# Moving ScalarE roundings ahead of a PSUM copy, and one sigmoid and one finishing step inside a pair loop, in the input projection of a hybrid encoder layer

## The chip, the cores and the metric

The kernel runs on one core of a Trainium2 chip. The metric is the device time in microseconds (us), the median over runs. TensorE (PE) multiplies, VectorE (DVE) and ScalarE (ACT) work on tiles in SBUF and PSUM, GpSimd (POOL) issues stores, SyncE (SP) issues loads.

## The reference

One encoder layer over 1024 prompt tokens and 256 sample tokens, all in float32. What matters here is its first product:

```
h = rms_norm(x, g_mix);  proj = h @ w_in        # (1280, 1024) @ (1024, 4096)
hq, hf_fwd, hf_bwd, hi, hg, dq, dk, dv = split(proj)      # eight groups of 512 columns
q_hg = silu(hq);  gate = silu(hg)
f = lb + (1 - lb) * sigmoid(hf);  lf = log(f);  k = 1 - f       # for hf_fwd and for hf_bwd
```

After it come a gated linear scan (HGRN2), differential attention, cross attention to 256 memory tokens, and a mixture of experts. None of that is changed.

## The kernel before

The function `front` computes the projection. Each float32 operand is split into a rounded high part and the low rest, and each product is three matmuls (`product3`, lines 113 to 115). ACT writes the high part and DVE subtracts it to get the low part.

**The steps.** The groups that are stored by token (`v`, `g`, `dv`) take 15 steps, n = 0 to 14, of two token tiles each: 48 matmuls of 512 columns into one of two PSUM halves, `acc[:, n % 2]`. PE may begin step n when the half has been read (`acc_read[n % 2]` at n // 2). In the steps of `dv`, n = 10 to 14, it is ACT that reads it, in `copy_out(n)` (line 516).

**The preparation of the pairs.** The other groups are stored by column. Ten pairs p = 0 to 9 (`q` 0 and 1, `f_fwd` 2 and 3, `f_bwd` 4 and 5, `dq` 6 and 7, `dk` 8 and 9) of 256 columns are computed as a two by two block product with seven products. They need four sums of token blocks, S1 to S4. DVE forms one with three additions over 128x2048 (`combine`, lines 709 to 713), ACT rounds it (`round_s`, line 526) and DVE subtracts (`low_s`, line 718). During steps 10 to 14 these are made, along with the eight weight slots of pair 0 (`round_slot` on ACT, line 538; `low_slot` on DVE, line 733). All engines run their instructions in the order in which the code lists them, with semaphores between them.

**The pairs.** For pair p, PE does eight slots in order, among them slots for the sample tokens (256 columns wide, into `x_t`). Before slot 7 it waits for `u3_done` of the same pair, since `p4_ps` and `p7_ps` are one bank: DVE must have added `p7_ps` to `partial` (`make_u3`, line 753). Meanwhile ACT and DVE make the slots of pair p + 1 and finish the chunks of pair p. Five chunks, c = 0 to 4, go through `clamp(p, c)` on DVE (line 797), `sigmoid(p, c)` on ACT (exponential, logarithm, exponential on lines 561 to 565, and for pairs 2 to 5 the logarithm of line 574 too), and `finish(p, c)` on DVE (line 805, or 808 for pairs 2 to 5). Pairs 6 to 9 have no sigmoid. `round_next(p, i)` is the rounding of slot i of pair p + 1; slots 4 and 7 wait for differences that DVE forms in `prepare(p + 1, 4)` (lines 745 and 746). The order on ACT for one p is:

```
copy_p1; sigmoid(p - 1, 3); sigmoid(p - 1, 4); round_next 0, 1; sigmoid(p, 0);
round_next 2, 3; sigmoid(p, 1); round_next 4, 5; copy_sample; round_next 6; sigmoid(p, 2); round_next 7
```

Of the kernel before, what the change touches and what calls it, by code (L numbers as in the profile page):

```python
# [171 lines left out]
def front(nc, tag, sources, gain, hg_lb, lam_vecs, ident, eps, lb, one_minus_lb, lb_minus_one, lam, weight, out,  # L172
# [26 lines left out]
    first_step = [g * tiles for g in range(len(BY_TOKEN))]  # L199
# [12 lines left out]
    S1, S3, S2, S4 = range(1, 5)  # L212
    with Mem(nc, tag) as m:
# [93 lines left out]
        def wait_pair_raw(eng, p):  # L307
            if p == 0:
                eng.wait_ge(first_pair_in, 16)
            else:  # L310
                eng.wait_ge(pair_in[p % 2], 16 * ((p + 1) // 2))
# [29 lines left out]
        with nc.Block() as block:  # L341
# [118 lines left out]
            def _(act):  # L460
# [16 lines left out]
                def find_mem_rstd(j):  # L477
                    t = NT + j
                    act.wait_ge(x_in[0], 16 * (NT // 2 + j + 1))
                    act.wait_ge(turned, t)  # L480
                    act.activation(xn[0][:], x[0][:], ACT.Square, accum_out=ss[:, t:t + 1])
                    act.drain()
                    act.activation(rstd[:, t:t + 1], ss[:, t:t + 1], ACT.Ln, scale=1.0 / D, bias=eps[:, 0:1])
                    act.drain()
                    act.activation(rstd[:, t:t + 1], rstd[:, t:t + 1], ACT.Exp, scale=-0.5).then_inc(rstd_done, 1)
# [38 lines left out]
                def round_s(i):  # L524
                    act.wait_ge(s_raw_done, i)
                    act.activation(s[i][:, 0], s_raw[i][:], ACT.Copy).then_inc(s_high_done, 1)

                def round_slot(p, i):
                    if i == 0:
                        wait_pair_raw(act, p)  # L530
                    if p:
                        act.wait_ge(slot_used, 8 * (p - 1) + i + 1)
                    elif i == 0:
                        act.wait_ge(mm_done, first_step[2])
                    made = {2: 2, 3: 1, 4: 3, 7: 4}
                    if i in made:
                        act.wait_ge(t_done, 4 * p + made[i])
                    act.activation(slot[:, i, 0], slot_source(p, i), ACT.Copy).then_inc(slot_high_done, 1)

                def round_next(p, i):  # L540
                    if p < last_pair:
                        round_slot(p + 1, i)
# [7 lines left out]
                def copy_sample(p):  # L550
                    act.wait_ge(sample_ready, p + 1)
                    wait_chunk_free(act, p, 2)
                    act.activation(chunk_of[:, 2], sample_ps(p), ACT.Copy, scale=scale_of(p)).then_inc(sample_copied, 1)

                def sigmoid(p, c):
                    if not 0 <= p < sig_pairs:
                        return
                    n = chunk_no(p, c)
                    part = sig[:, n % 3]
                    act.wait_ge(part_clamp_done, n + 1)  # L560
                    act.activation(part, part, ACT.Exp, scale=-1.0)
                    act.drain()
                    act.activation(part, part, ACT.Ln, bias=one[:, 0:1])
                    act.drain()
                    act.activation(part, part, ACT.Exp, scale=-1.0).then_inc(part_sig_done, 1)
                    if pairs[p][0] in GATES:
                        g = gate_no(p, c)
                        act.drain()
                        if g == 0:
                            act.wait_ge(lb_done, 1)  # L570
                        if g >= 3:
                            act.wait_ge(lf_stored[g % 3], 16 * (g // 3))
                        for h, cols in heads_of(p, c):
                            done = act.activation(staged_lf[:, g % 3, cols], part[:, cols], ACT.Ln,
                                                  scale=one_minus_lb[:, h:h + 1], bias=lb[:, h:h + 1])
                        done.then_inc(lf_done, 1)
# [26 lines left out]
                for n, (g, kind, j) in enumerate(steps):  # L603
                    if n < tiles:
                        continue
                    if n in chunk_in_step:
                        round_chunk(chunk_in_step[n])
                    if first_mem < n <= first_mem + mem_tiles:
                        round_mem(n - first_mem - 1)
                    if first_mem <= n < first_mem + mem_tiles:  # L610
                        find_mem_rstd(n - first_mem)
                    if kind in SILUS:
                        wide_sigmoid(n)
                    else:
                        copy_out(n)
                    if n == first_step[2]:
                        round_s(S1)
                    if n == first_step[2] + 1:
                        for i in range(8):
                            round_slot(0, i)  # L620
                        round_s(S3)
                    if n == first_step[2] + 3:
                        round_s(S2)
                    if n == first_step[2] + 4:
                        round_s(S4)
                    for r in out_rounds.get(n, ()):
                        round_out(r)

                for p in range(len(pairs)):
                    copy_p1(p)  # L630
                    sigmoid(p - 1, 3)
                    sigmoid(p - 1, 4)
                    round_next(p, 0)
                    round_next(p, 1)
                    sigmoid(p, 0)
                    round_next(p, 2)
                    round_next(p, 3)
                    sigmoid(p, 1)
                    round_next(p, 4)
                    round_next(p, 5)  # L640
                    if p == last_pair:
                        act.wait_ge(next_in, 32)
                        act.wait_ge(slot_used, 8 * p + 3)
                        for i, (_, high_of, _) in enumerate(next_split):
                            act.activation(high_of[:], next_raw[:, i], ACT.Copy).then_inc(next_high_done, 1)
                    copy_sample(p)
                    round_next(p, 6)
                    sigmoid(p, 2)
                    round_next(p, 7)

            @block.vector
            def _(dve):
# [83 lines left out]
                def prepare(p, *which):  # L736

                    if p > last_pair:
                        return
                    for i in which:  # L740
                        if i == 1:
                            differences(p)
                        if i == 4:
                            dve.drain()
                            dve.tensor_tensor(spread[:, 1], weights_of(p, 1, 0), spread[:, 1], ALU.subtract)
                            dve.tensor_tensor(spread[:, 0], weights_of(p, 1, 1), weights_of(p, 0, 1),
                                              ALU.subtract).then_inc(t_done, 1)
                            dve.drain()
                            dve.sem_inc(t_done, 1)
                        low_slot(p, i)  # L750
# [131 lines left out]
                for p in range(len(pairs)):  # L882
                    finish(p - 1, 3)
                    prepare(p + 1, 0)
                    finish(p - 1, 4)
                    prepare(p + 1, 1)
                    make_c11(p)
                    clamp(p, 0)
                    make_u2(p)
                    prepare(p + 1, 2)  # L890
                    make_u3(p)
                    make_c22_u4(p)
                    clamp(p, 1)
                    prepare(p + 1, 3)
                    finish(p, 0)
                    prepare(p + 1, 4, 5)
                    clamp(p, 2)
                    if p == last_pair:
                        for i, (_, high_of, low_of) in enumerate(next_split):
                            dve.wait_ge(next_high_done, i + 1)  # L900
                            dve.tensor_tensor(low_of[:], next_raw[:, i], high_of[:].bitcast(F32), ALU.subtract)
                    make_c12(p)
                    clamp(p, 3)
                    finish(p, 1)
                    prepare(p + 1, 6)
                    make_c21(p)
                    clamp(p, 4)
                    finish(p, 2)
                    prepare(p + 1, 7)
# [2468 lines left out]
```

## Time and profile before

| | |
|---|---|
| median of 3 runs | 2049.55 us (2048.66 to 2050.41) |
| profiled execution, its own time | 2048.66 us |
| its span in the trace | 2046.9 us |
| granted TensorE clock, mean | 0.984 |
| PE busy | 1956.1 us, 96% |
| DVE busy | 1489.8 us, 73% |
| ACT busy | 1237.7 us, 60% |
| first matmul of pair 0 | 201.22 us from the start of the span |
| first matmul after `front` | 460.38 us |

Times in the trace count from the start of the span. The timeline gives each instruction's start, then its duration, then engine, line, operation and tiles; in brackets stands how long its engine sat idle before it, and what released it. A matmul is recorded as 0.39 us long, but they follow each other at 0.227 us.

### The profile page before, as it was taken

To read this page: it belongs to the slowest core of one execution; us is meant where nothing else is said; L and a number is where in the kernel's file an instruction comes from. 1 tells how busy PE (TensorE), PEld (TensorE's weight loads), DVE (VectorE), ACT (ScalarE), POOL (GpSimd) and SP (SyncE) were. 2 spreads that over 40 slices of the span, in tenths; PEclk is the share of its full clock that TensorE was granted. 3 is DMA by queue.
4 is the path that set the end of the run, shared out by engine and by line. 5 is a ranking of instruction groups with operands and counts; after the bars stand their busy time and mean duration, and the time that the engine had idled before them with its cause. 6 is when DMAs were issued, how large, how long until landed. Compare 5 with 4: busy or idle time off the path is not lost. (4 is left out here: it accounts for less than half of the span.)

```text
span 2046.9 us, 31859 instructions
## 1 busy us (share of the span) xinstructions
PE 1956.1 (96%) x11162; PEld 1618.9 (79%) x11162; DVE 1489.8 (73%) x2050; ACT 1237.7 (60%) x1974; POOL 307.8 (15%) x394
## 2 busy tenths in 40 slices
PE   7989999999999899999998999999999999999983
PEld 6878887888888676778887888887888888888871
DVE  5447766639999588887311455579999999999976
ACT  5443566418787598643222333337888888888863
POOL 0220012200000121111000000011222332222210
PEclk9999999999999999999999999989999999999997
DMA  6493233446554541343335322448999999999988
GB/s 209 165 308 109 93 124 134 160 170 200 175 173 156 188 160 60 97 144 133 117 115 164 124 103 73 165 170 317 383 384 382 380 379 375 384 383 395 376 314 321
DMA packets 178389, 448.27 MB, mean 219 GB/s; under 512 B 21152, under 2 KB 100384, under 8 KB 151648
## 3 DMA queue, kind: packets, MB, share of 16 engines
q1 hardware_dynamic: 146032, 347.48, 47.6%
q0 software_dynamic: 32240, 99.25, 13.1%
q8 instruction: 70, 1.15, 0.2%
q14 instruction: 47, 0.39, 0.1%
HBM read 366.46 MB, written 94.90 MB: 225 GB/s over the span
## 5 line engine op out<-in xcount | busy, mean ns | idle before, releaser
L113 PE MATMUL cross_ot_ps<-w_w_high,cross_o_high 128*128 128x512 f32 x544 | 219.8, 404 | 2.1 <-DVE w_w_low L2933 1.6
L115 PE MATMUL cross_ot_ps<-w_w_high,cross_o_low 128*128 128x512 f32 x544 | 213.3, 392 | 0.0
L2933 DVE TENSOR_TENSOR cross_low_up<-cross_raw_up,w_w_high 128x2048 fp32r<-128x2048 f32 x68 | 152.8, 2289 | 12.3 <-ACT w_w_high L2717 12.2
L2933 DVE TENSOR_TENSOR cross_low_down<-cross_raw_down,w_w_low 128x2048 fp32r<-128x2048 f32 x68 | 152.7, 2288 | 1.8 <-ACT w_w_low L2717 1.7
L2933 DVE TENSOR_TENSOR w_w_low<-cross_raw_gate,w_w_high 128x2048 fp32r<-128x2048 f32 x68 | 152.2, 2278 | 0.0
L2717 ACT ACTIVATE w_w_high<-cross_raw_up 128x2048 fp32r<-128x2048 f32 x68 | 126.2, 1907 | 0.3 <-issue 0.3
L2717 ACT ACTIVATE w_w_low<-cross_raw_down 128x2048 fp32r<-128x2048 f32 x68 | 126.2, 1907 | 0.0
L2717 ACT ACTIVATE w_w_high<-cross_raw_gate 128x2048 fp32r<-128x2048 f32 x68 | 126.1, 1902 | 0.0
L113 PEld LDWEIGHTS cross_ot_ps<-w_w_high,cross_o_high 128*128 128x128 f32 x544 | 102.9, 189 | 28.5 <-DVE w_w_low L2933 7.1
L115 PEld LDWEIGHTS cross_ot_ps<-w_w_high,cross_o_low 128*128 128x128 f32 x544 | 102.7, 189 | 22.2
L113 PE MATMUL cross_out_ps<-w_w_low,cross_ht 128*128 128x512 f32 x272 | 109.5, 403 | 5.6 <-DVE cross_low_down L2933 5.6
L114 PE MATMUL cross_ot_ps<-w_w_low,cross_o_high 128*128 128x512 f32 x272 | 107.0, 393 | 0.0
L115 PE MATMUL cross_out_ps<-w_w_low,cross_ht 128*128 128x512 f32 x272 | 107.0, 393 | 0.0
L114 PE MATMUL cross_out_ps<-cross_low_down,cross_ht 128*128 128x512 f32 x272 | 106.6, 392 | 0.0
L114 PE MATMUL cross_ot_ps<-cross_low_up,cross_o_high 128*128 128x512 f32 x272 | 106.0, 390 | 0.0
L2627 POOL COPY cross_result<-cross_result_i 128x1 int32 x32 | 39.7, 1239 | 332.0 <-ACT cross_x L2753 332.0
L1782 DVE CUSTOM_DVE_ANT_0 amq_score<-amq_banks,amq_bias 128x1024 f32<-128x1024 f32 x64 | 75.8, 1221 | 14.2 <-PE amq_banks L2177 13.9
L2631 POOL DMA_INDIRECT y_rows<-cross_x,cross_result x32 | 81.9, 2559 | 27.0 <-POOL cross_result L2627 27.0
L2744 ACT ACTIVATE cross_o_high<-cross_score_ps 128x1024 fp32r<-128x1024 f32 x34 | 34.9, 1028 | 82.4 <-PE cross_score_ps L3252 82.4
L2196 PEld LDWEIGHTS amq_banks<-amq_v,amq_attn_t 128*128 128x128 f32 x512 | 59.6, 191 | 25.4 <-ACT amq_attn_t L1985 20.8
L1977 ACT ACTIVATE amq_prob<-amq_score,amq_least 128x1024 f32<-128x1024 f32 x64 | 72.6, 1137 | 4.9 <-DVE amq_least L1782 4.9
L113 PEld LDWEIGHTS cross_out_ps<-w_w_low,cross_ht 128*128 128x128 f32 x272 | 51.5, 189 | 23.6 <-issue 10.4
(515 smaller groups left out, 5570.2 us busy)
## 6 DMA issues: line engine op xcount, KB each, us to landing
cross_raw_gate<-in_w_gate_dram SPq DMA_DIRECT2D x68, 1024.0 KB, 7.0
cross_raw_down<-in_w_down_dram SPq DMA_DIRECT2D x68, 1024.0 KB, 7.7
cross_raw_up<-in_w_up_dram SPq DMA_DIRECT2D x68, 1024.0 KB, 9.0
front_pair_raw<-in_w_in_dram SPq DMA_DIRECT2D x9, 1024.0 KB, 7.0
cross_y_kept<-y_rows SPq DMA_DIRECT2D x16, 512.0 KB, 9.4
front_raw<-in_w_in_dram SPq DMA_DIRECT2D x10, 512.0 KB, 5.3
k_t<-front_staged POOLq DMA_DIRECT2D x20, 256.0 KB, 2.4
lf_t<-front_staged_lf POOLq DMA_DIRECT2D x20, 256.0 KB, 3.2
```

Source lines behind the costliest of these rows:

```text
L113: pe.matmul(out, lhs[0], rhs[0], start=first, stop=False)
L114: pe.matmul(out, lhs[0], rhs[1], start=False, stop=False)
L115: return pe.matmul(out, lhs[1], rhs[0], start=False, stop=last)
L1782: done = dve.tensor_tensor_reduce(out=score[:, u, c], in0=score_ps[:, c], in1=bias[:, h, col:col + SEQ_P], scale=1.0, scalar=3.0e38, op0=A ...
L1977: done = act.activation(prob[:, u, c], score[:, u, c], ACT.Exp, scale=-1.0, bias=least[:, u, c:c + 1], accum_out=total[:, n % 4, c:c + 1])
L2196: last = pe.matmul(o_ps[:, u, 0:P], attn_t[:, c * P:(c + 1) * P], v[:, c, h * P:(h + 1) * P], start=(c == 0), stop=(c == NT_P - 1))
L2627: pool.tensor_copy(result[u][:], result_i[:, ds(n, 1)]).then_inc(result_done, 1)
L2631: pool.indirect_dma_start(out=y_rows, in_=y[:, u], in_offset=None, out_offset=bass.IndirectOffsetOnAxis(ap=at, axis=0), bounds_check=2 * T ...
L2717: act.activation(w_high[s][:, cols], raw[s][:, cols], ACT.Copy).then_inc(w_high_done[s], 1)
L2744: act.activation(x_high[:, u].rearrange("p k t -> p (k t)"), xt_ps[:], ACT.Copy).then_inc(x_high_done, 1)
L2933: dve.tensor_tensor(w_low[s][:, cols], raw[s][:, cols], w_high[s][:, cols].bitcast(F32), ALU.subtract).then_inc(w_low_done[s], 1)
```

## The change

Three orders are changed; no instruction is added or taken away.

```diff
@@ ScalarE, steps n = 10 to 14
                     if first_mem <= n < first_mem + mem_tiles:
                         find_mem_rstd(n - first_mem)
+                    if n == first_step[2]:
+                        round_s(S1)
+                    if n == first_step[2] + 1:
+                        round_s(S3)
+                        for i in range(8):
+                            round_slot(0, i)
+                    if n == first_step[2] + 3:
+                        round_s(S2)
+                    if n == first_step[2] + 4:
+                        round_s(S4)
                     if kind in SILUS:
                         wide_sigmoid(n)
                     else:
                         copy_out(n)
-                    if n == first_step[2]:
-                        round_s(S1)
-                    if n == first_step[2] + 1:
-                        for i in range(8):
-                            round_slot(0, i)
-                        round_s(S3)
-                    if n == first_step[2] + 3:
-                        round_s(S2)
-                    if n == first_step[2] + 4:
-                        round_s(S4)
@@ ScalarE, the pair loop
                     round_next(p, 2)
                     round_next(p, 3)
-                    sigmoid(p, 1)
                     round_next(p, 4)
                     round_next(p, 5)
...
                     copy_sample(p)
+                    sigmoid(p, 1)
                     round_next(p, 6)
@@ VectorE, the pair loop
                     make_u2(p)
-                    prepare(p + 1, 2)
+                    finish(p, 0)
+                    prepare(p + 1, 2, 3)
                     make_u3(p)
                     make_c22_u4(p)
                     clamp(p, 1)
-                    prepare(p + 1, 3)
-                    finish(p, 0)
                     prepare(p + 1, 4, 5)
```

`first_step[2]` is 10, the first step of `dv`.

## Rows read from the trace of the kernel before

**Rows 1.** Waits, 160 to 465 us: engine, line, releaser, us in total, times, longest

```profile
PE front_acc L113 <- DVE front_partial L753: 5.4, 3, 3.0
```

**Rows 2.** Timeline of PE: firsts of steps 12 and 14, and of slots in pairs

```profile
167.56 0.39 PE L113 MATMUL front_acc<-front_w_high,front_bottom 128*128 128x512 f32 x1
...
190.19 0.50 PE L113 MATMUL front_acc<-front_w_high,front_sample 128*128 128x512 f32 x1 [0.71 <-ACT front_staged L516]
...
201.22 0.39 PE L113 MATMUL front_acc<-front_top,front_slot 128*128 128x512 f32 x1
...
223.34 0.39 PE L113 MATMUL front_acc<-front_bottom,front_slot 128*128 128x512 f32 x1
...
226.06 0.39 PE L113 MATMUL front_acc<-front_top,front_slot 128*128 128x512 f32 x1
...
299.36 0.47 PE L113 MATMUL front_acc<-front_bottom,front_slot 128*128 128x512 f32 x1 [1.33 <-DVE front_partial L753]
...
302.19 0.39 PE L113 MATMUL front_acc<-front_top,front_slot 128*128 128x512 f32 x1
...
327.47 0.77 PE L113 MATMUL front_acc<-front_bottom,front_slot 128*128 128x512 f32 x1 [3.00 <-DVE front_partial L753]
...
331.88 0.40 PE L113 MATMUL front_acc<-front_top,front_slot 128*128 128x512 f32 x1
...
358.03 0.39 PE L113 MATMUL front_acc<-front_top,front_slot 128*128 128x512 f32 x1
```

**Rows 3.** Busy time by stretch; after the engines: granted clock, DMA share, GB/s

```profile
320.00:330.00 10.00, 7.00 (x33) 5.72 (x32) 6.62 (x12) 4.51 (x8) 0.13 (x1) 0.87 0.15 54
```

**Rows 4.** Timeline of ACT during steps 10 to 14

```profile
156.98 1.01 ACT L516 ACTIVATE front_staged<-front_acc 128x1024 f32<-128x1024 f32 x1
170.17 1.92 ACT L526 ACTIVATE front_s<-front_s_raw 128x2048 fp32r<-128x2048 f32 x1 [12.18 <-DVE front_s_raw L713]
171.99 1.01 ACT L516 ACTIVATE front_staged<-front_acc 128x1024 f32<-128x1024 f32 x1
...
187.33 1.90 ACT L526 ACTIVATE front_s<-front_s_raw 128x2048 fp32r<-128x2048 f32 x1
189.14 1.92 ACT L516 ACTIVATE front_staged<-front_acc 128x1024 f32<-128x1024 f32 x2
```

**Rows 5.** Timeline of ACT in the pairs, pair 4 above all

```profile
233.12 0.62 ACT L561 ACTIVATE front_sig<-front_sig 128x512 f32<-128x512 f32 x1
...
256.89 0.62 ACT L561 ACTIVATE front_sig<-front_sig 128x512 f32<-128x512 f32 x1
...
283.02 0.62 ACT L561 ACTIVATE front_sig<-front_sig 128x512 f32<-128x512 f32 x1
...
311.13 0.62 ACT L561 ACTIVATE front_sig<-front_sig 128x512 f32<-128x512 f32 x1
...
325.21 1.13 ACT L538 ACTIVATE front_slot<-front_spread 128x512 fp32r<-128x512 f32 x2
329.26 0.63 ACT L561 ACTIVATE front_sig<-front_sig 128x512 f32<-128x512 f32 x1 [2.92 <-DVE front_sig L797]
...
332.19 0.61 ACT L538 ACTIVATE front_slot<-front_spread 128x512 fp32r<-128x512 f32 x1
...
338.41 0.57 ACT L548 ACTIVATE front_partial<-front_acc 128x512 f32<-128x512 f32 x1
338.89 0.62 ACT L561 ACTIVATE front_sig<-front_sig 128x512 f32<-128x512 f32 x1
```

**Rows 6.** Timeline of DVE in pair 4

```profile
326.64 0.69 DVE L753 SCALAR_TENSOR_TENSOR front_partial<-front_acc,front_partial 128x512 f32<-128x512 f32 x1
...
328.80 0.43 DVE L797 TENSOR_SCALAR front_sig<-front_staged 128x512 f32<-128x512 f32 x1
329.14 0.69 DVE L733 TENSOR_TENSOR front_slot<-front_spread,front_slot 128x512 fp32r<-128x512 f32 x1
...
330.99 0.68 DVE L746 TENSOR_TENSOR front_spread<-front_pair_raw 128x512 f32<-128x512 f32 x1
```

## The prediction, made before the changed kernel ran

> **What bounds the kernel.** I read the page first: TensorE is busy for 96% of the span, so a change in the order of the other engines counts only where TensorE has to wait. The view of the waits, cut to the stretch from 160 to 465 us in which the change lies, shows how little there is: the reader is to see that three waits on DVE's `partial` make 5.4 us [rows 1], and the timeline adds one of 0.71 us on ACT's copy, at the start of step 14 [rows 2]. Everything else runs at the pace of the matmuls: 48 in a step at 0.227 us are 10.88 us; one pair takes 226.06 - 201.22 = 24.84 us, and reaches slot 7 at 223.34 - 201.22 = 22.12 us [rows 2]. Pairs 0, 1 and 2 keep this pace, so pair 3 starts at 201.22 + 3 x 24.84 = 275.74. Pair 6 starts at 358.03 instead of 275.74 + 3 x 24.84 = 350.26: pairs 3, 4 and 5 lose 7.77 us. That is the three pauses, and the clock after the longest. The granted clock is 0.87 from 320 to 330 us [rows 3], a mixture of the two levels of 1.2 and 2.4 GHz. The twelve matmuls after the 3.00 us pause take 331.88 - 327.47 = 4.41 us for 2.72, a loss of 1.7; after the pause of 1.33 us they take 302.19 - 299.36 = 2.83, a loss of 0.1 [rows 2].
>
> So I looked for two things: which instruction the edits put between TensorE and what it waits for, and how long the loop between ACT and DVE takes per pair.
>
> **Edit 1, ACT in steps 10 to 14.** Before, ACT copies step 10 out at 156.98, and only then waits 12.18 us for DVE's last addition of S1, so that the rounding starts at 170.17 [rows 4]. After, `round_s(S1)` stands ahead of that copy. Nothing makes the addition earlier: DVE had been waiting for the stores of `out_split`, on which the copy has no bearing. The rounding stays at 170.17, the next instruction on ACT starts at 171.99, and this is now the copy of step 10, done at 173.00 as the copy in that place was. TensorE needs it for step 12 (`acc_read[0]` at 6), which was to start at 167.56 [rows 2]. It starts at 173.05: 5.5 us late.
>
> Then step 11. ACT rounds S3 (1.9 us) when DVE has added it up, and then the eight slots, paced by DVE's subtractions and differences as before; they end so that the next instruction starts at 187.33, where the rounding of S3 stood [rows 4]. Now the copy of step 11 starts there, and ends 1.01 us later at 188.34. TensorE needs it for step 13. Step 12 would end at 173.05 + 10.88 = 183.93 plus what the clock costs after the pause (1.7 as after the pause of 3.00), 185.6. So there is a second wait, of some 2.7 us, and step 13 starts at 188.38 whatever the clock did before. The 0.71 us ahead of step 14 goes away, since the copy of step 12 now comes at 188.3 and not at 189.14. Steps 13 and 14 take 2 x 10.88 plus the clock's loss after the second wait. That pause is between the ones of 1.33 and 3.00, so the loss is between 0.1 and 1.7, and I take 1.0. Pair 0 starts at 188.38 + 21.76 + 1.0 = 211.1 instead of 201.22: **9.9 us late**, with bounds of 9.0 and 10.6. The roundings of S2 and S4 ahead of the copies of steps 13 and 14 cost nothing here: S2 is rounded about when step 13 ends, and pair 0 needs the copy of step 14 only for its fourth slot. If those sums were late, TensorE would wait in pair 0 for `s_ready` too. Queued behind the held copies are POOL's stores of `dv_rows` and, since `mm_done` comes later, SP's loads for pairs 1 and 2; both move with TensorE.
>
> **Edits 2 and 3, the pair loop.** I measure ACT's loop from the first exponential of `sigmoid(p - 1, 3)`. Pair 4 to pair 5 is 338.89 - 311.13 = 27.76 us, pair 3 to pair 4 is 28.11 [rows 5]. Both are longer than TensorE's 24.84, and this is why TensorE waits. In the loop, DVE's `u3` starts at 326.64, 15.51 after the loop's start, and ends at 327.33, which releases slot 7 at 327.47 [rows 2, 6].
>
> After: `finish(p, 0)` fits into the time in which DVE waits for ACT's rounding of slot 2 at 325.21 [rows 5] and costs nothing. The subtraction of slot 3 moves ahead of `u3`. In the old order it stood behind `clamp(p, 1)` at 329.14, and the rows there follow each other at 0.6 us [rows 6]. So `u3` comes 0.6 later, and so does the clamp: 329.4. The differences that slot 4 needs ended at 330.99 + 0.68 = 331.67; with 0.6 more ahead of the clamp and 1.2 less behind it (and a drain of 0.1 in its place) they end at 331.2. The rounding of slot 4 was at 332.19 behind a sigmoid, and is now at 331.25: 0.9 earlier only, while the sigmoid of 2.93 us (332.19 - 329.26) now comes after it. ACT waited 2.92 us for the clamp; it now waits for the differences, 5 us. From the rounding of slot 4, the four short instructions of 0.52, 0.52, 0.48 and 0.52, the sigmoid of 2.93, `sigmoid(p, 2)` of 3.21, slot 7 of 0.52 and the copy of 0.48 lead to the next start at 340.43 for 338.89: **the loop becomes 1.54 us longer, 29.3 us**. In pair 2 the same walk gives 283.02 - 256.89 = 26.13 before and 27.7 after. In pairs 0 and 1, without the second logarithm, 256.89 - 233.12 = 23.77 before and 24.8 after [rows 5], just TensorE's pace.
>
> Against this stands that TensorE starts pair 0 late, and so the loop less far behind it. Before, the loop's start in pair 2 was 256.89 - 250.90 = 6.0 us after TensorE's. After, it is as near as it can be: twelve matmuls (2.72), 0.2, and the copy at 338.41 to 338.89 (0.48) [rows 5], 3.4 us. Then pair 3: 3.4 + 27.7 - 24.84 = 6.2 us behind. Slot 7 of pair 5 can start no sooner than 6.2 + 2 x 29.3 + 15.51 + 0.6 + 0.69 + 0.14 = 81.8 us after TensorE's start of pair 3; without waits it would be 2 x 24.84 + 22.12 = 71.8. That is 10.0 us lost, and behind it 1.2 of clock (bounds again 0.1 and 1.7): 11.2 for 7.77 before, so **3.4 us more**, with bounds of 2.3 and 3.9. The clock's losses at the earlier pauses don't add to it, since they shorten the next pause. If the loads for pair 1 hold the loop up, it starts up to 1.9 us further behind, and the upper bound is 5.8. Pairs 6 to 9 have hardly any work for ACT and catch up.
>
> **The sum.** 9.9 + 3.4 = 13.3 us. After `front` every stage starts on TensorE's end, so the rest moves as a whole. The profiled execution's own time of 2048.66 becomes 2062.0; the median of 2049.55, 0.9 above it, becomes 2062.9.
>
> [...]
>
> **Rivals.**
> - *The pair loop doesn't get longer* (the sigmoid's place is taken up by ACT's idle time, as the edit would suggest). Then only the nearer start counts: 3.4 + 26.13 - 24.84 = 4.7 behind, slot 7 of pair 5 at 4.7 + 2 x 27.76 + 16.34 = 76.6 for 71.8, with the clock 6.0 lost for 7.77. Total 9.9 - 1.8 = 8.1, 2057.7 us. Against it: the differences, which ACT then waits for, are only 0.5 us earlier.
> - *The loop starts as far behind as before*, 6.0 or more, because of the loads. Then 2.6 us more, 2065.5.
> - *The pair loop's pauses vanish altogether*, if rounding slots 4 and 5 early were what `u3` hangs on: 9.9 - 7.8 = 2.1, 2051.7 us. Against it: `u3` waits for slot 2's subtraction, which is not earlier.
> - *Not slower: the copy of step 10 is not held.* Place: ACT, ahead of step 12. It decides if DVE's last addition of S1 ends before the copy could start at 156.98 and the slots' roundings before 178.4. Then 1.0 us is gained ahead of step 14, and with a loop of the old length and the nearer start another 1.8: 2046.7 us, 0.14% under the time before. Against it: the addition ends 13 us too late, and no edit touches what it waits for.
>
> **How the numbers follow.** Forecast 0.62; loop not longer 0.13; loop as far behind 0.15; pauses gone 0.04; copy not held 0.03; and 0.03 left for what I don't see, most of it on the side of faster. A measurement of this kernel can tell about 0.2% (4 us) from no change. The pauses gone (0.10% slower) and the copy not held both count as the same. So slower 0.90, same 0.07, faster 0.03. The range: the low bounds give 9.0 + 2.3 = 11.3, so 2060.9, the high ones 10.6 + 5.8 = 16.4, so 2066.0. I stretch it down to 2058, which the shorter loop nearly reaches, and up to 2067.
>
> **What would show it.** In the profile after: a wait of TensorE for ACT's line of `copy_out` near 173 us and a second near 188, of 5.3 and some 2.5 us, and none ahead of step 14; the rounding of S1 still at 170.2; pair 0's first matmul near 211; ACT's loop at 29.3 us in pairs 3 and 4; pauses ahead of slot 7 of about 1, 4 and 2.5 us in pairs 3 to 5, released by `partial`; the first matmul after `front` near 473.7. It is wrong if step 12 starts near 167.6, or if the loop stays at 27.8.

## The result, and the profile after

The changed kernel took 2064.74 us (median of 3 runs, 2061.48 to 2066.44) for 2049.55: a ratio of 1.0073, with a 95% interval from 1.0054 to 1.0091. It is slower, as forecast, and the time lies in the range. Its profiled execution took 2061.51 us, with a span of 2059.7 for 2046.9, 12.8 us more. The forecast was 13.3. The medians lie further apart than the profiled executions, 15.2 us; the runs of one kernel scatter by 4 to 5 us, and a part of the experiments is about where.

What TensorE waited for from 160 to 480 us, in the profile after:

```profile
PE front_acc L113 <- DVE front_partial L753: 7.9, 3, 4.2
PE front_acc L113 <- ACT front_staged L516: 7.8, 2, 5.3
```

The waits for ACT's copy grew from 0.7 to 7.8 us, and those for `partial` from 5.4 [rows 1] to 7.9. The timeline of PE, with the rows that answer to [rows 2]:

```profile
172.84 0.80 PE L113 MATMUL front_acc<-front_w_high,front_bottom 128*128 128x512 f32 x1 [5.33 <-ACT front_staged L516]
...
188.20 0.50 PE L113 MATMUL front_acc<-front_w_high,front_bottom 128*128 128x512 f32 x1 [2.48 <-ACT front_staged L516]
...
199.21 0.39 PE L113 MATMUL front_acc<-front_w_high,front_sample 128*128 128x512 f32 x1
...
210.09 0.39 PE L113 MATMUL front_acc<-front_top,front_slot 128*128 128x512 f32 x1
...
259.77 0.39 PE L113 MATMUL front_acc<-front_top,front_slot 128*128 128x512 f32 x1
...
284.61 0.39 PE L113 MATMUL front_acc<-front_top,front_slot 128*128 128x512 f32 x1
...
307.82 0.47 PE L113 MATMUL front_acc<-front_bottom,front_slot 128*128 128x512 f32 x1 [0.92 <-DVE front_partial L753]
...
337.14 0.76 PE L113 MATMUL front_acc<-front_bottom,front_slot 128*128 128x512 f32 x1 [4.23 <-DVE front_partial L753]
...
366.48 0.47 PE L113 MATMUL front_acc<-front_bottom,front_slot 128*128 128x512 f32 x1 [2.77 <-DVE front_partial L753]
...
370.80 0.50 PE L113 MATMUL front_acc<-front_top,front_slot 128*128 128x512 f32 x1
...
473.27 0.64 PE L113 MATMUL hgrn_acc<-mem_high,mem_next_high 128*128 128x512 f32 x1 [2.83 <-PEq L91]
```

Step 12 starts at 172.84 for 167.56, step 13 at 188.20, and step 14 at 199.21 without a wait. Pair 0 starts at 210.09 for 201.22: 8.9 us. From the start of pair 3 to that of pair 6 it is 370.80 - 284.61 = 86.19 us, which is 11.7 more than three times 24.84; before it was 7.8 more. The first matmul after `front` comes at 473.27 for 460.38: 12.9 us, and that is the whole difference of the spans. The granted clock (after the engines) in the stretch with the longest pause of the pairs is 0.84 for 0.87 [rows 3]:

```profile
330.00:340.00 10.00, 5.77 (x21) 4.38 (x20) 7.17 (x13) 3.84 (x6) 1.07 (x2) 0.84 0.21 80
```

ACT in the steps, answering to [rows 4]:

```profile
155.83 1.06 ACT L522 ACTIVATE front_out_high<-front_out_raw 128x1024 fp32r<-128x1024 f32 x1 [5.38 <-DMA front_out_raw<-in_w_out_dram]
169.97 1.91 ACT L526 ACTIVATE front_s<-front_s_raw 128x2048 fp32r<-128x2048 f32 x1 [13.08 <-DVE front_s_raw L713]
171.78 1.00 ACT L516 ACTIVATE front_staged<-front_acc 128x1024 f32<-128x1024 f32 x1
176.90 1.93 ACT L526 ACTIVATE front_s<-front_s_raw 128x2048 fp32r<-128x2048 f32 x1 [4.11 <-DVE front_s_raw L713]
...
187.15 1.92 ACT L516 ACTIVATE front_staged<-front_acc 128x1024 f32<-128x1024 f32 x2
```

The copy of step 10 was at 156.98 and is now at 171.78, behind a rounding that waits 13.08 us. The copies of steps 11 and 12 follow each other from 187.15. ACT in the pairs, answering to [rows 5] (the loop of pair 2 starts at 263.19, that of pair 4 at 320.22 and the next at 349.54):

```profile
263.19 0.62 ACT L561 ACTIVATE front_sig<-front_sig 128x512 f32<-128x512 f32 x1
...
320.22 0.62 ACT L561 ACTIVATE front_sig<-front_sig 128x512 f32<-128x512 f32 x1
...
334.27 1.13 ACT L538 ACTIVATE front_slot<-front_spread 128x512 fp32r<-128x512 f32 x2
340.38 0.63 ACT L538 ACTIVATE front_slot<-front_spread 128x512 fp32r<-128x512 f32 x1 [4.97 <-DVEq L748]
...
341.91 0.62 ACT L561 ACTIVATE front_sig<-front_sig 128x512 f32<-128x512 f32 x1
...
349.54 0.62 ACT L561 ACTIVATE front_sig<-front_sig 128x512 f32<-128x512 f32 x1
```

In pair 2 the loop starts 263.19 - 259.77 = 3.42 us behind TensorE, for the 3.4 of the prediction. In pair 4 it takes 29.32 us for 27.76. The wait of 2.92 us for the clamp is gone, and one of 4.97 for DVE's differences stands in its place, with the sigmoid behind it at 341.91. DVE in the same pair, answering to [rows 6]:

```profile
333.50 0.55 DVE L808 TENSOR_SCALAR front_staged<-front_sig,kept_lb_minus_one,kept_one_minus_lb 128x512 f32<-128x512 f32 x1 [1.41 <-ACT front_sig L565]
334.92 1.29 DVE L733 TENSOR_TENSOR front_slot<-front_spread,front_slot 128x512 fp32r<-128x512 f32 x2 [0.86 <-ACT front_slot L538]
336.30 0.69 DVE L753 SCALAR_TENSOR_TENSOR front_partial<-front_acc,front_partial 128x512 f32<-128x512 f32 x1
...
339.60 0.69 DVE L746 TENSOR_TENSOR front_spread<-front_pair_raw 128x512 f32<-128x512 f32 x1
```

`finish(p, 0)` at 333.50 lies in DVE's wait for slot 2, as predicted, with 0.86 us to spare. Two subtractions (334.92, x2) now stand ahead of `u3`, at 336.30 - 320.22 = 16.08 us from the loop's start for 15.51. The differences end at 340.29, 20.1 from it, for 20.5.

### The profile page after: what moved, and what is told of

The parts are those of the page before. It is cut to its first block and busy times, and to the rows that moved or that the text cites. A ratio compares the mean times of both kernels' runs of the same rounds, so it can differ in the third digit from the quotient of the medians.

```text
span 2059.7 us, 31859 instructions
## 1 busy us (share of the span) xinstructions
PE 1958.7 (95%) x11162; PEld 1620.1 (79%) x11162; DVE 1491.5 (72%) x2050; ACT 1237.7 (60%) x1974; POOL 307.7 (15%) x394
```

## The experiments

Times below are medians, and a ratio, with its 95% interval, is against runs of the kernel before that were taken beside it (medians of 2050.07, 2049.66 and 2049.53 us). "Front end" is the first matmul after `front`, 460.38 us before. It is read from one profiled execution. For what the edits do inside `front` it is the better measure, for a reason that the first run shows; it says nothing of what follows.

**The change once more.**

> The changed kernel once more. Its profiled execution took 2061.5 us, 12.9 more than the one before, and its timed runs had a median of 2064.7, 15.2 more. If the clock's loss after the middle pauses differs from run to run (bounds 0.1 and 1.7 us at each of two), five rounds scatter between 2061.5 and 2065 and the ratio is 1.006 to 1.0075. If the profiled execution was a lucky one, they all lie at 2064 and above.

2062.35 us (2061.68 to 2066.63), ratio 1.0061, 1.0046 to 1.0076. The profiled execution took 2066.63, 5.1 us longer than the one above. Its `front` ended at 473.29, as the other one did at 473.27. So the difference between these two executions arises behind `front`. These five runs lie in two bunches, near 2062 and near 2066; of the three above, one (2064.74) lies between. I had looked for the scatter in the pauses of the pairs, and it is elsewhere.

That the two front ends agree to 0.02 us is partly chance. In this execution steps 12 and 13 and pair 0 start some 0.55 us later (pair 0 at 210.65), and behind the third pause of the pairs the clock costs 0.1 us where it cost 1.7. What evens it out is that slot 7 of pair 6 waits here for `u3`, which it did not do above:

```profile
367.04 0.47 PE L113 MATMUL front_acc<-front_bottom,front_slot 128*128 128x512 f32 x1 [2.60 <-DVE front_partial L753]
...
392.95 0.47 PE L113 MATMUL front_acc<-front_bottom,front_slot 128*128 128x512 f32 x1 [0.81 <-DVE front_partial L753]
```

Pair 0 itself starts between 200.50 and 201.51 us in the five profiles in which the orders of the steps are those of before. So a difference of a microsecond between two front ends can be chance, and where the clock behind a pause is in it, one of 1.6.

The 5 us of the whole execution lie further on. The largest part lies where the experts start: the first transposes there (before 1380 us) came 0.8 us later in the longer execution, the first matmul of the experts at 1384.9 for 1382.0, and the second block's transposes at 1400.43 for 1396.47. There, busy time and granted clock (the column behind POOL) in the execution of 2061.5 us:

```profile
1380.00:1384.00 4.00, 4.00 (x21) 3.50 (x21) 3.78 (x6) 0.00 (x0) 0.00 (x0) 0.67 0.88 329
1384.00:1388.00 4.00, 4.00 (x18) 3.25 (x17) 3.88 (x3) 0.00 (x0) 0.00 (x0) 0.90 0.75 264
1388.00:1392.00 4.00, 4.00 (x24) 3.39 (x23) 2.78 (x6) 2.03 (x3) 0.99 (x1) 1.00 0.96 371
```

and in the one of 2066.6:

```profile
1381.00:1385.00 4.00, 4.00 (x21) 4.00 (x20) 3.67 (x6) 0.00 (x0) 0.00 (x0) 0.50 0.93 340
1385.00:1389.00 4.00, 4.00 (x11) 3.13 (x11) 3.99 (x2) 0.00 (x0) 0.00 (x0) 0.50 0.71 255
1389.00:1393.00 4.00, 4.00 (x19) 3.23 (x17) 0.92 (x5) 0.00 (x0) 0.00 (x0) 0.89 0.96 383
```

A granted clock of 0.50 is the level of 1.2 GHz. TensorE stays at it for the whole of the first two stretches, eight microseconds, in the longer execution; in the shorter one the two stretches that answer to them, 1 us earlier, have 0.67 and 0.90, some 3.5 us at that level, and 18 matmuls for 11 in the second. The profiled execution of the run with edits 2 and 3 alone, below, is a long one too (2062.28 us), and has a clock of 0.50 there from 1376 to 1384 us. What decides between the two, and the last 1.2 us of the difference, which come in the experts themselves, wasn't tried.

**Edit 1 alone.**

```diff
+                    if n == first_step[2]:
+                        round_s(S1)
+                    if n == first_step[2] + 1:
+                        round_s(S3)
+                        for i in range(8):
+                            round_slot(0, i)
...
                         copy_out(n)
```

The change's first hunk is in whole (the part for steps 10 and 11 is shown); the two others are left out.

> Edit 1 alone. My theory: pair 0 starts 8.9 us late, as after the whole change (waits of 5.3 and 2.5 us for ACT's copies ahead of steps 12 and 13), and ACT's loop keeps its 27.8 us but starts 3.4 us behind TensorE, so that pairs 3 to 5 lose 6.0 instead of 7.8: 7.1 us more, 2056.7. Rival, that the pair loop has nothing to do with where it starts: 8.9 more with the pauses as before, 2058.5.

2056.77 us (ratio 1.0029, 1.0019 to 1.0040); front end 468.07, 7.7 us more. Pair 0 starts at 210.15, 8.9 late, and ACT's loop starts pair 3 nearer to TensorE, 4.7 us behind it for 7.3. Pauses are left in pairs 4 and 5 only:

```profile
333.81 0.47 PE L113 MATMUL front_acc<-front_bottom,front_slot 128*128 128x512 f32 x1 [2.03 <-DVE front_partial L753]
...
361.58 0.77 PE L113 MATMUL front_acc<-front_bottom,front_slot 128*128 128x512 f32 x1 [2.65 <-DVE front_partial L753]
```

They make 4.7 us for 5.4 before. The late start gives 1.2 us back in the pairs; I had expected 1.8. The rival, that the pauses stay as they were, is out: the one in pair 3 is gone.

**The parts of edit 1, each alone.**

First only the rounding of S1 goes ahead of the copy:

```diff
+                    if n == first_step[2]:
+                        round_s(S1)
                     if kind in SILUS:
                         wide_sigmoid(n)
                     else:
                         copy_out(n)
-                    if n == first_step[2]:
-                        round_s(S1)
```

> Of edit 1 only the part of step 10: the rounding of S1 ahead of the copy of step 10. My theory: the copy at 172, step 12 starts 5.5 us late, the copies of steps 11 and 12 are then in time, pair 0 starts near 207.3, 6.1 late; with the nearer start of the loop 4.3 more, 2053.9. Rival, that the second wait is a consequence of the first: pair 0 as late as after the whole change, 8.9, with 2056.7.

2054.35 us (1.0022, 1.0012 to 1.0033). One wait of 5.38 us, pair 0 at 207.73, front end 464.30, 3.9 more. Step 13 starts without a wait and pair 0 is 6.5 us late, not 8.9, so the second wait of the changed kernel is not a consequence of the first.

Then only the roundings of step 11 go ahead of it:

```diff
+                    if n == first_step[2] + 1:
+                        round_s(S3)
+                        for i in range(8):
+                            round_slot(0, i)
                     if kind in SILUS:
                         wide_sigmoid(n)
                     else:
                         copy_out(n)
...
-                    if n == first_step[2] + 1:
-                        for i in range(8):
-                            round_slot(0, i)
-                        round_s(S3)
```

> Of edit 1 only the part of step 11: the rounding of S3 and the eight slot roundings ahead of the copy of step 11; the rounding of S1 stays behind the copy of step 10. My theory: the copy of step 11 again starts near 187.3, so step 13 starts near 188.4 whatever came before; instead of two waits there is one of 9.8 us, step 12 being on time, and pair 0 starts near 211.9 or, with less clock lost, 210.5: as late as with the whole of edit 1. With the loop's nearer start the time is 7 to 9 us more, 2056.5 to 2058.5. Rival, that each held copy costs its own wait: only the 2.5 us of the second, less the 1.8 of the nearer start, 2050.

2058.84 us (1.0043, 1.0030 to 1.0057), front end 469.20, 8.8 more, with one long wait ahead of step 13 and pair 0 at 212.60, where I had expected 211.9 at most:

```profile
188.05 0.79 PE L113 MATMUL front_acc<-front_w_high,front_bottom 128*128 128x512 f32 x1 [9.87 <-ACT front_staged L516]
```

Each part alone has its wait, but they don't add up: 6.5 and 11.4 us at pair 0 against 8.9 for both. Step 13 starts near 188 in each kernel that holds the copy of step 11, and a late step 12 only fills that wait. The rest is clock: from step 13 to pair 0 it costs 212.60 - 188.05 - 21.76 = 2.8 us behind the long wait, and 0.1 behind the one of 2.48 us in the changed kernel. The rival with a wait of 2.5 us alone is out.

**Edits 2 and 3 without edit 1.**

The steps are as before; the change's second and third hunk are in:

```diff
-                    sigmoid(p, 1)
...
                     copy_sample(p)
+                    sigmoid(p, 1)
@@ VectorE
                     make_u2(p)
-                    prepare(p + 1, 2)
+                    finish(p, 0)
+                    prepare(p + 1, 2, 3)
                     make_u3(p)
                     make_c22_u4(p)
                     clamp(p, 1)
-                    prepare(p + 1, 3)
-                    finish(p, 0)
```

> Edits 2 and 3 without edit 1. My theory: pair 0 at 201.2 as before, ACT's loop 29.3 us in pairs 3 and 4 and starting 10 us behind TensorE in pair 3, so that pairs 3 to 5 lose about 15 instead of 7.8: 7.2 us more, 2056.8, and more than the 4.0 that the loop costs behind edit 1. Rival, that the loop's cost is the same wherever it starts: 4.0 more, 2053.6.

2061.96 us (1.0046, 1.0031 to 1.0062); front end 468.75, 8.4 us more, where I had expected 7.2. Behind edit 1 the same two edits cost 473.27 - 468.07 = 5.2 us (the 4.0 of the expectation is what is left of them after the 1.2 that the late start gives back). The loop takes 29.34 us in pairs 3 and 4, as in the changed kernel. It starts further behind TensorE, so that there are six pauses from pair 0 to pair 6, 11.2 us together. The rival of a fixed cost is out: what the longer loop costs depends on how far behind it starts. The median is 11.9 us above the one before, not 8.4: four of its six runs lie at 2061.8 to 2062.5 and two at 2056.3 and 2057.1, two bunches as with the changed kernel.

**Edit 2 alone, and edit 3 alone.**

First only the sigmoid moves:

```diff
                     round_next(p, 3)
-                    sigmoid(p, 1)
...
                     copy_sample(p)
+                    sigmoid(p, 1)
```

> Edit 2 alone: on ACT, sigmoid(p, 1) behind copy_sample(p). My theory: the differences for slot 4 end at 331.7 as before, so its rounding comes only 0.5 us earlier while a sigmoid of 2.9 follows it: ACT's loop 29.8 us in pairs 3 and 4, u3 at 15.5 us from its start as before. Pairs 3 to 5 lose 16 us instead of 7.8: 8.6 more, 2058.2, worse than both pair edits together. Rival, that edit 3 is the costly one because it delays u3: then 2 us or less here.

2059.78 us (1.0044, 1.0030 to 1.0057); front end 470.77, 10.4 us more, 1.8 above what I expected and 2.0 above both edits together. The pauses make 13.3 us for their 11.2. By the medians it is the other way round, 2059.78 for 2061.96; those of both edits together have the upper bunch in them. In pair 4, whose loop on ACT starts at 317.96, the rounding of slot 4 waits 5.43 us, and the loop takes 29.79. Pair 2 has a pause of 1.11 us already, and pair 6 one of 1.22; I had counted the longer loop only from pair 1 on, and it begins in pair 0: the loop of pair 1 starts at 234.75 us for 233.12. The rows of pair 4:

```profile
338.59 0.63 ACT L538 ACTIVATE front_slot<-front_spread 128x512 fp32r<-128x512 f32 x1 [5.43 <-DVEq L748]
...
347.75 0.61 ACT L561 ACTIVATE front_sig<-front_sig 128x512 f32<-128x512 f32 x1
```

Then only DVE's order changes:

```diff
                     make_u2(p)
-                    prepare(p + 1, 2)
+                    finish(p, 0)
+                    prepare(p + 1, 2, 3)
                     make_u3(p)
                     make_c22_u4(p)
                     clamp(p, 1)
-                    prepare(p + 1, 3)
-                    finish(p, 0)
```

> Edit 3 alone: on DVE, finish(p, 0) and the subtraction of slot 3 ahead of u3. My theory: u3 and clamp(p, 1) come 0.6 us later, ACT's loop grows from 27.8 to 28.4, pairs 3 to 5 lose 11 us instead of 7.8: 3.2 more, 2052.7. Rival, that the later u3 alone counts and the loop does not grow: 0.6 us in all, 2050.2.

2051.56 us (1.0010, 1.0001 to 1.0019); front end 463.78, 3.4 us more; the median is 1.9 us above the one before. The loop is 28.36 us in pair 4, for 27.76, so the rival of a loop that does not grow is out. So the moved sigmoid is the costly edit, and the DVE edit takes 0.4 us of the loop back when both are there, since it brings the differences forward.

**A loop that is shorter.** The kernel before, with `u3` and all that hangs on it ahead of DVE's wait for slot 2:

```diff
                     make_u2(p)
+                    make_u3(p)
+                    make_c22_u4(p)
+                    clamp(p, 1)
                     prepare(p + 1, 2)
-                    make_u3(p)
-                    make_c22_u4(p)
-                    clamp(p, 1)
                     prepare(p + 1, 3)
```

> The kernel before, with another order on DVE in the pair loop: make_u3, make_c22_u4 and clamp(p, 1) right behind make_u2, ahead of the subtraction of slot 2. My theory: u3 no longer waits for ACT's rounding of slot 2 and ends 3.6 us sooner in the loop, and ACT no longer waits 2.9 us for clamp(p, 1), so its loop is 24.8 us, TensorE's own pace: no pause in pairs 3 to 5, 7.8 us less, 2041.8. Rival, that something else (the differences for slot 4, or slot_used) takes the place of the clamp and the loop stays above 26: then 2 to 5 less.

2042.65 us (2039.97 to 2046.02), ratio 0.9959, 0.9946 to 0.9973; front end 452.69, 7.7 us less. The pairs have no pause, and no other wait takes the place of the clamp's, as the rival had it. ACT in pair 4:

```profile
305.38 0.62 ACT L561 ACTIVATE front_sig<-front_sig 128x512 f32<-128x512 f32 x1
...
319.45 1.14 ACT L538 ACTIVATE front_slot<-front_spread 128x512 fp32r<-128x512 f32 x2
320.49 0.62 ACT L561 ACTIVATE front_sig<-front_sig 128x512 f32<-128x512 f32 x1
...
330.11 0.62 ACT L561 ACTIVATE front_sig<-front_sig 128x512 f32<-128x512 f32 x1
```

and DVE:

```profile
317.43 0.69 DVE L753 SCALAR_TENSOR_TENSOR front_partial<-front_acc,front_partial 128x512 f32<-128x512 f32 x1 [0.16 <-PE front_acc L115]
...
319.60 0.43 DVE L797 TENSOR_SCALAR front_sig<-front_staged 128x512 f32<-128x512 f32 x1
320.10 1.29 DVE L733 TENSOR_TENSOR front_slot<-front_spread,front_slot 128x512 fp32r<-128x512 f32 x2
```

`u3` at 12.05 us from the loop's start, the clamp done before ACT asks for it, the sigmoid right behind slot 3, and a loop of 24.73 us, just under TensorE's 24.84. `u3` now waits for TensorE (0.16) and no longer TensorE for `u3`.

**The same with the rounding of S3 ahead of the slots,** but every copy ahead of the roundings.

```diff
                     if n == first_step[2] + 1:
+                        round_s(S3)
                         for i in range(8):
                             round_slot(0, i)
-                        round_s(S3)
```

> The kernel with u3 early (no pause in pairs 3 to 5, first matmul after the front at 452.7), and besides, on ACT behind the copy of step 11, the rounding of S3 ahead of the eight slot roundings; all copies stay ahead of the roundings. My theory: the copy of step 12 then starts at 187.3 instead of 189.1, TensorE's wait of 0.6 ahead of step 14 is gone, pair 0 starts near 200.3 and the first matmul after the front comes near 451.7: 8.8 us less than before, 2041. Rival, that the rounding of S3 ahead of the slots delays the slots and with them pair 0: pair 0 later than 201.3.

2042.44 us (2039.67 to 2044.93), ratio 0.9964, 0.9950 to 0.9977. Against the run without it the time can't tell; the trace can: no wait ahead of step 14, pair 0 at 200.34 for 201.30, front end 451.73 for 452.69, with step 12 at the same time in both (167.69 and 167.73). Its front end is the earliest of all. Both versions are faster than the kernel before and the changed one; which of the two is the faster isn't shown.

**Edit 1 with that loop.** DVE's order is that of `u3` early, and the change's first hunk is in:

```diff
+                    if n == first_step[2]:
+                        round_s(S1)
...
                         copy_out(n)
...
@@ VectorE
                     make_u2(p)
+                    make_u3(p)
+                    make_c22_u4(p)
+                    clamp(p, 1)
...
```

> Edit 1 as in the changed kernel, with the pair loop of u3 early. My theory: the held copies cost TensorE what they cost in the changed kernel, pair 0 near 210.1, and nothing in the loop changes that, as it has no pause left: first matmul after the front at 461.5, 1.1 us more than before, 2050.8. Rival, that the loop takes up part of the delay where it has slack: below 459 and no different from u3 early by more than 6 us.

2054.24 us (1.0023, 1.0014 to 1.0032); front end 460.84, 8.2 us more than with `u3` early alone. Pair 0 starts at 209.45, 8.2 us later too. Nothing in the pairs takes the delay up. The time is not what I expected, 2050.8: the front end lies 0.5 us behind the one before, and the median 4.7 us above it. The profiled execution took 2050.59 us and is the shortest of the eleven (up to 2056.91); no trace was kept of a longer one, so what the others lose, and why here more than before, stays open.

## Why the prediction held, point by point

- *Edit 1 holds the copy of step 10 behind the rounding of S1.* Shown: step 12 is 5.28 us late, predicted 5.5; the run with S1 alone has the same wait, 5.38 us for 5.33.
- *The copy of step 11 then sets step 13, whatever the first wait was.* Shown by the run with the roundings of step 11 alone: 188.05, against 188.20 after the change.
- *Pair 0 9.9 us late.* It was 8.9, by the term that I had set at 1.0 between bounds of 0.1 and 1.7: behind the wait of 2.48 us step 13 took 11.01 for 10.88, a loss of 0.1. Step 13 also started 0.18 us sooner than the walk had it, so that 8.9 lies just under the lower bound of 9.0.
- *ACT's loop becomes 1.54 us longer and starts nearer to TensorE.* Shown: 29.32 to 29.34 for the predicted 29.3. That it is DVE's differences that slot 4's rounding waits for, with the sigmoid behind it, is what the runs with edit 2 alone (29.79) and edit 3 alone (28.36) show, and the rival of a loop that doesn't get longer is out. So is the one of vanishing pauses: they vanish when `u3` itself moves ahead of slot 2, not when slot 4's rounding does. The third, a loop held up by the loads, is out by its start in pair 2, 3.42 us behind TensorE.
- *3.4 us in the pairs.* It was 12.9 - 8.9 = 4.0, just above the bound of 3.9 for a loop that isn't held up. Slot 7 of pair 5 starts 366.48 - 284.61 = 81.87 us after pair 3, predicted 81.8, so the chain was right. The clock behind it was the term off: 370.80 - 366.48 = 4.32 us for 2.72 and 0.1 after it, 1.7 where I took 1.2, its upper bound. I had also put the pairs behind pair 5 at nothing. In the second execution the clock costs 0.1 there, and pair 6 takes back most of the gain by waiting 0.81 us for `u3`: the long loop reaches into pair 6, and a cheap clock behind pair 5 can't bring the pairs down to the lower bound of 2.3.
- *After `front` everything moves as a whole.* It holds for the two profiled executions, 12.9 us at the front's end and 12.8 in the span. It doesn't hold in general: the second execution of the changed kernel has the same front end and a span 5.2 us longer, and with edit 1 and `u3` early the front end is that of before and the median 4.7 us higher.
- What I had no term for is the spread of the runs by 4 to 5 us. Of the 5.2 us between two executions of the changed kernel 3.2 lie in the experts' start.

The mechanism was right in both parts. That the sum came so near has luck in it. The two terms of the clock missed in opposite directions, -0.9 and +0.5, which is why it came out at 12.9 for 13.3. In the second execution the same 12.9 is made of other parts, 9.4 at pair 0 and 3.5 in the pairs. And the medians of the two sets of runs are 15.2 and 12.3 us above those before; the range had room for the first only by its terms for loads that hold the loop up, which they did not, and by the stretch at its upper end.

## What to carry to other kernels

An engine that runs its instructions in order and serves two others wants them in the order in which their inputs come: here a rounding that waits 13 us held up a copy that had been ready all along. Where two engines take turns in a loop, measure the loop from one start to the next against the pace of the engine that they feed; moving a long instruction behind a wait that it used to cover made the loop longer here, and moving short ones ahead of a wait (`u3` and the clamp, 7.7 us) made it shorter. Delays at two points don't add up where one later instruction sets the time for both. And a mark inside the trace tells what a change did ahead of it, to a microsecond or two of chance; the time of the whole has to be measured besides.

## What the hardware showed that I had not expected

What a pause costs in clock is not a matter of its length alone. Two executions of the changed kernel have the same pause in pair 4. In one the matmuls behind it are slow at once (0.63 us recorded for 0.39):

```profile
337.14 0.76 PE L113 MATMUL front_acc<-front_bottom,front_slot 128*128 128x512 f32 x1 [4.23 <-DVE front_partial L753]
337.70 0.63 PE L114 MATMUL front_acc<-front_bottom,front_slot 128*128 128x512 f32 x1
```

In the other the first ones run at full speed, and the level falls behind them:

```profile
337.71 0.47 PE L113 MATMUL front_acc<-front_bottom,front_slot 128*128 128x512 f32 x1 [4.24 <-DVE front_partial L753]
338.01 0.40 PE L114 MATMUL front_acc<-front_bottom,front_slot 128*128 128x512 f32 x1
338.25 0.39 PE L115 MATMUL front_acc<-front_bottom,front_slot 128*128 128x512 f32 x1
338.48 0.56 PE L113 MATMUL front_acc<-front_bottom,front_slot 128*128 128x512 f32 x1
338.84 0.63 PE L114 MATMUL front_acc<-front_bottom,front_slot 128*128 128x512 f32 x1
```

Pauses of 2.48 us (after the change, ahead of step 13) and 2.65 us (edit 1 alone, pair 5) differ too: the one cost 0.1 us of clock, the other 365.71 - 361.58 - 2.72 = 1.4. The widest contrast is between the run with edit 3 alone, pair 3, and the one with edit 2 alone, pair 5:

```profile
299.93 0.60 PE L113 MATMUL front_acc<-front_bottom,front_slot 128*128 128x512 f32 x1 [2.00 <-DVE front_partial L753]
```

```profile
364.08 0.47 PE L113 MATMUL front_acc<-front_bottom,front_slot 128*128 128x512 f32 x1 [3.07 <-DVE front_partial L753]
```

The pause of 2.00 us cost 304.34 - 299.93 - 2.72 = 1.7 us, and the one of 3.07 cost 366.92 - 364.08 - 2.72 = 0.1. What decides it, no run here shows. The Trainium skill, "TensorE: Matmul & The Clock Gate", Part 1, says that the number of slow matmuls at a kernel's start differs between runs of one kernel. The traces here show the same in the middle of a kernel: behind the pause of pair 5 seven matmuls are recorded at 0.63 us in one execution of the changed kernel (pause of 2.77 us) and none in the other (2.60 us), and the stretches at the lower level at the experts' start are under 4 and over 8 us long.
